# Attention steps of the first token tile placed ahead of the second tile's heads in a one-core transformer kernel

## What is computed

```python
n = _rms_norm(h, attn_norm[layer])
proj = n @ w_in[layer]
c_q, c_kv, k_rope, dq, dk, dv = jnp.split(proj, IN_SPLITS, axis=-1)
...
q = (_rms_norm(c_q, q_norm) @ w_uq).reshape(b, l, MLA_HEADS, MLA_QK_DIM)
kv = (_rms_norm(c_kv, kv_norm) @ w_ukv).reshape(b, l, MLA_HEADS, MLA_NOPE_DIM + MLA_V_DIM)
k_nope, v = kv[..., :MLA_NOPE_DIM], kv[..., MLA_NOPE_DIM:]
...
q = _rms_norm(q, qk_norm_q)
k = _rms_norm(k, qk_norm_k)
q = jnp.concatenate([q[..., :MLA_NOPE_DIM], _rope(q[..., MLA_NOPE_DIM:], pos)], axis=-1)
...
s = jnp.einsum('bqhd,bkhd->bhqk', qb, k) * scale
p = _causal_softmax(s, q_pos, pos)
return jnp.einsum('bhqk,bkhd->bqhd', p.astype(v.dtype), v)
...
mod = (c_act @ w_ada[l] + b_ada[l]).reshape(B, N_SUBLAYERS, N_MOD, D_MODEL)
```

## Time and profile before

| | us |
|---|---|
| median of 3 runs | 1675.62 |
| lowest and highest run | 1672.96 and 1677.15 |
| the profiled execution, its own time | 1671.1 |
| its span | 1669.2 |
| TensorE busy in it | 1290.4 |
| VectorE busy in it | 1021.7 |
| ScalarE busy in it | 402.0 |
| POOL busy in it | 572.4 |

### The profile page before, as it was taken

The page is one execution under the profiler, slowest core; times in us unless marked ns, Lnnn a source line. Parts: engine busy times, 40 slices in busy tenths (PEclk is TensorE's granted clock), DMA queues, the critical chain, the costliest instruction groups (busy, mean ns, idle before and its releaser), DMA issues.

```text
span 1669.2 us, 17159 instructions
## 1 busy us (share of the span) xinstructions
PE 1290.4 (77%) x6237; PEld 923.5 (55%) x6237; DVE 1021.7 (61%) x1897; ACT 402.0 (24%) x702; POOL 572.4 (34%) x626
## 2 busy tenths in 40 slices
PE   6987899687665554545565559999979889999997
PEld 3435667354222222222222226989969889799996
DVE  4575347977668577565655562767656554356655
ACT  1124312221001000110111101333334451144332
POOL 2100002677767767567777773101010000000000
PEclk9995589899777777777777779999989999899999
DMA  9634114899999999999999995777746435327561
GB/s 331 244 101 151 51 51 177 338 373 373 375 380 387 365 377 395 393 384 360 376 371 376 355 365 194 259 261 270 271 151 231 148 103 200 127 94 234 170 207 63
DMA packets 179707, 435.42 MB, mean 261 GB/s; under 512 B 13881, under 2 KB 84610, under 8 KB 179638
## 3 DMA queue, kind: packets, MB, share of 16 engines
q0 software_dynamic: 84384, 306.26, 48.4%
q1 hardware_dynamic: 94214, 126.18, 22.5%
q10 hardware_dynamic: 1040, 2.10, 0.4%
HBM read 433.44 MB, written 2.14 MB: 261 GB/s over the span
## 4 chain that ended last, share of the span: by engine, by line
PE 55%; DMA 14%; POOL 11%; DVE 10%; issue 7%; ACT 3%; SPq 0%; DVEq 0%; POOLq 0%; ACTq 0%
PE quad L1334 13%; PE quad_a L1292 7%; DMA arena<-in_peer_v_dram,arena 6%; PE quad_a L1348 6%; POOL ring L722 6%; PE quad L1292 5%; POOL arena L722 5%; PE quad_a L1077 5%; PE quad_a L1415 5%; DMA ring<-in_peer_v_dram,arena 4%; PE quad_a L1483 2%; PE quad L1152 2%; PE quad_a L1473 2%; DMA ring<-in_ffn_w_gu_dram 2%; PE quad L1235 1%
## 5 line engine op out<-in xcount | busy, mean ns | idle before, releaser
L1292 PE MATMUL quad_a<-arena 128*128 128x512 f32 x384 | 202.5, 692 | 158.6 <-DMA arena<-in_peer_v_dram,arena 158.6
L1292 PE MATMUL quad<-ring,arena 128*128 128x512 f32 x360 | 186.4, 681 | 119.3 <-DMA ring<-in_peer_v_dram,arena 119.3
L1292 PEld LDWEIGHTS quad_a<-arena 128*128 128x128 f32 x384 | 84.6, 226 | 275.9 <-issue 275.7
L722 POOL DMA_INDIRECT ring<-in_peer_u_dram,arena x136 | 138.5, 1018 | 247.5 <-PE quad L1152 178.2
L1334 PE MATMUL quad<-u_hi,w_hi 128*128 128x256 f32 x704 | 200.5, 285 | 2.7 <-DVE u_lo L1773 2.7
L1292 PEld LDWEIGHTS quad<-ring,arena 128*128 128x128 f32 x360 | 78.0, 222 | 224.6 <-issue 224.6
L1334 PE MATMUL quad<-u_lo,w_hi 128*128 128x256 f32 x704 | 200.4, 285 | 0.0
L1334 PE MATMUL quad<-u_hi,w_lo 128*128 128x256 f32 x704 | 200.2, 284 | 0.0
L1741 DVE TENSOR_TENSOR w_lo<-ring,w_hi 128x2048 fp32r<-128x2048 f32 x66 | 150.8, 2290 | 66.9 <-ACT w_hi L900 66.6
L675 POOL DMA_DIRECT2D arena<-in_w_ada_dram x48 | 25.4, 532 | 448.1 <-DVE arena L1542 445.5
L1873 DVE CUSTOM_DVE_ANT_0 arena<-ring,quad 128x1024 f32<-128x1024 f32 x128 | 154.8, 1221 | 25.2 <-DMA ring<-in_peer_u_dram,arena 16.9
(11 more groups left out here) (302 smaller groups left out, 2197.0 us busy)
## 6 DMA issues: line engine op xcount, KB each, us to landing
ring<-in_ffn_w_gu_dram SPq DMA_DIRECT2D x44, 1024.0 KB, 9.4
arena<-in_w_ada_dram POOLq DMA_DIRECT2D x48, 512.0 KB, 5.7
ring<-in_ffn_w_down_dram SPq DMA_DIRECT2D x22, 1024.0 KB, 4.9
ring<-in_w_mix_in_dram SPq DMA_DIRECT2D x20, 1024.0 KB, 6.3
ring<-in_w_ada_dram POOLq DMA_DIRECT2D x24, 512.0 KB, 5.5
arena<-in_peer_w_query_dram SPq DMA_DIRECT2D x4, 2048.0 KB, 8.2
arena<-in_w_in_dram SPq DMA_DIRECT2D x3, 2048.0 KB, 14.2
arena<-in_w_out_dram SPq DMA_DIRECT2D x2, 2048.0 KB, 10.3
```

The costliest lines, as they stand in the source:

```text
L722: gp.indirect_dma_start(out=rows_of(n), out_offset=None, in_=t["peer_" + kind][0], in_offset=bass.IndirectOffsetOnAxis(ap=expert[tt][:, sl ...
L1292: last = te.matmul(sum_side[tt][:, cols], diag[:, i % DIAGS], rows_of(n)[:, cols], start=(slot == pe_slots[0]), stop=(slot == pe_slots[-1] ...
```

## The change

Attention of tile 0 is begun once the latent heads of tiles 0 and 2 are turned, and other work is put between its steps.

- TensorE: after `cT` come the latent heads of tiles 0 and 2 at once, then `dq` of both tiles, `dv` of tile 0, and the turning of the latent heads of tiles 0 and 2. Then the loop begins. In pass 0, after the scores, stands `dv` of tile 1. In pass 1, after `o` of step 0, stand `dv` of tile 2, the turning of all differential heads, and the latent heads of tile 1. In pass 3, after `o` of step 2, stands the turning of tile 1's latent heads. The quarters of `keys` move from passes 1 to 4 to passes 3 to 6.
- VectorE: the latent heads of q0, k0 and k2 are done first, then those of `dq`. The sums of q1 and k1 stand at the end of pass 1, their scaling and rotation at the end of pass 2.
- ScalarE: its copies and roots follow.
- `v_row`, the rotation's scratch rows and `tmp` move to other places. The `w_ada` slices of this stage have three buffers instead of four, and their groups on VectorE are 6, 12 and 6, so 18 stand ahead of the copy of `cT` instead of 14. POOL's wait for the biases now stands ahead of the 19th load.
- SP: the load of `g_ffn` (512 KB) moves from the start to behind step 5 of attention; the loads of `w_out` and of the query weights wait for tile 1's heads.

```diff
-        v_row = area(arena, W2, 3 * MH * MV).rearrange("p (t n) -> p t n", t=3)
-        rot = area(arena, W2 + 3 * MH * MV, 3 * MH * ROPE).rearrange("p (s h c) -> p s h c", s=3, h=MH)
+        v_row = area(ring, 8960, 3 * MH * MV).rearrange("p (t n) -> p t n", t=3)
+        rot = [area(ring, at, MH * ROPE).rearrange("p (h c) -> p h c", h=MH) for at in (10496, 10752, 12032)]
         dv_row = area(arena, W2 + 2304, 3 * DH * DV).rearrange("p (t n) -> p t n", t=3)
...
-        tmp = area(ring, 4352, 1024)
+        tmp = area(ring, 11008, 1024)
...
-        ADA_BUFS = 4
-        ada_head = [area(ring, at, D) for at in (0, D, 2 * D, 9984)]
-        ada_late = [area(arena, LATE + D * i, D) for i in range(ADA_BUFS)]
+        ADA_HEAD, ADA_LATE = 3, 4
+        ada_bufs = [area(ring, D * i, D) for i in range(ADA_HEAD)] + [area(arena, LATE + D * i, D) for i in range(ADA_LATE)]
 
         def ada_buf(n):
 
-            return (ada_late if ADA[n][0] else ada_head)[n % ADA_BUFS]
+            return n % ADA_HEAD if n < 24 else ADA_HEAD + (n - 24) % ADA_LATE
+
+        def ada_turn(n):
+
+            return n // ADA_HEAD if n < 24 else (n - 24) // ADA_LATE
 
         def ada_count(s, columns):
...
         a_jobs = [("c", tt) for tt in range(3)] + [("rope", tt) for tt in range(3)] + [("dk", tt) for tt in range(3)]
-        a_jobs += [("dq", tt) for tt in range(QT)]
-        for tt in range(3):
+        for tt in (0, 2):
             a_jobs += [("q", tt, n) for n in range(2) if tt < QT] + [("kv", tt, n) for n in range(2)]
-        a_jobs += [("dv", tt) for tt in range(3)] + [("dkT", tt) for tt in range(3)] + [("dqT", tt) for tt in range(QT)]
-        for tt in range(3):
+        a_jobs += [("dq", tt) for tt in range(QT)] + [("dv", 0)]
+        for tt in (0, 2):
             a_jobs += [("qT", tt, n) for n in range(2) if tt < QT] + [("kT", tt, n) for n in range(2)]
+        a_jobs.append(("dv", 1))
         for i, (tt, g) in enumerate(STEPS):
-            if i < 4:
-                a_jobs.append(("keysT", i))
+            if 2 <= i < 6:
+                a_jobs.append(("keysT", i - 2))
             a_jobs += [("pT", i, m) for m in maps(g)]
+            if i == 0:
+                a_jobs += [("dv", 2)] + [("dkT", tt) for tt in range(3)] + [("dqT", tt) for tt in range(QT)]
+                a_jobs += [("q", 1, n) for n in range(2)] + [("kv", 1, n) for n in range(2)]
+            if i == 2:
+                a_jobs += [("qT", 1, n) for n in range(2)] + [("kT", 1, n) for n in range(2)]
 
         ADA_JOBS = ("columns", 0, 1)
...
             sp.dma_start(w_rope, w_in[:, :, C_ROPE:C_ROPE + ROPE]).then_inc(ld_rope_w, 16)
-            sp.dma_start(g_ffn, t["ffn_norm"].to_broadcast([P, D])).then_inc(ld_gffn, 16)
...
             sp.dma_start(keys, t["peer_sub_keys"][0].rearrange("h s n d -> n (h s) d")).then_inc(ld_keys, 16)
-            sp.wait_ge(a_full.sem, a_at["dqT", QT - 1] + 1)
-            sp.wait_ge(head_ready.sem, 1)
+            sp.wait_ge(a_full.sem, a_at["kv", 1, 1] + 1)
+            sp.wait_ge(head_ready.sem, 4)
             for n in range(2):
                 sp.dma_start(wo_half[n], w_out[:, :, n * 512:(n + 1) * 512]).then_inc(ld_wo, 16)
-            sp.wait_ge(a_full.sem, a_at["kT", 2, 1] + 1)
+            sp.wait_ge(a_full.sem, a_at["kT", 1, 1] + 1)
             load_query(1)
             sp.wait_ge(a_full.sem, a_at["keysT", 3] + 1)
             load_query(0)
+            sp.wait_ge(d_full.sem, d_at["o", 5] + 1)
+            sp.dma_start(g_ffn, t["ffn_norm"].to_broadcast([P, D])).then_inc(ld_gffn, 16)
             sp.wait_ge(d_full.sem, d_at["o", len(STEPS) - 1] + 1)
             load_query(2)
...
                     s, m, k = ADA[n]
-                    if n >= ADA_BUFS:
-                        pool.wait_ge(ada_used.sem, n - ADA_BUFS + 1)
+                    if ada_turn(n):
+                        pool.wait_ge(ada_used.sem, n - (ADA_LATE if s else ADA_HEAD) + 1)
                     src = t["w_ada_2"][0, k * P:(k + 1) * P, (3 * s + m) * D:(3 * s + m + 1) * D]
-                    gp.dma_start(ada_buf(n), src).then_inc(ld_ada[n % ADA_BUFS], 16)
+                    gp.dma_start(ada_bufs[ada_buf(n)], src).then_inc(ld_ada[ada_buf(n)], 16)
 
             def begin_sums(*sums_of):
...
             pool.wait_ge(d_full.sem, d_at["nT", 2, 1] + 1)
-            load_ada(*range(ADA_BUFS))
+            load_ada(*range(ADA_HEAD))
             bias_ready.step(pool, gp.memset(mask, 0.0))
             for tt in range(QT):
                 bias_ready.step(pool, gp.affine_select(out=mask[:, tt], in_=mask[:, tt], compare_op=ALU.is_ge, fill=NEG,
                                                        base=META + P * tt, pattern=[[-1, KEYS]], channel_multiplier=1))
...
 
-            load_ada(*range(10, 24))
+            load_ada(*range(18, 24))
...
+            evac_up(0)
+            evac_up(2)
+            evac_dq(0)
+            for name in (("q", 0), ("k", 0), ("k", 2)):
+                root(name, ROWS_OF.get(name, P))
+            evac_dq(1)
+            evac_dv(0)
+            evac_turned(0)
+            evac_turned(2)
+            for tt in range(QT):
+                root(("dq", tt))
...
+                if i == 0:
+                    evac_dv(1)
...
                     tt, g = STEPS[i - 1]
-                    if i < 5:
-                        n = i - 1
+                    if 3 <= i < 7:
+                        n = i - 3
                         evac(("keysT", n), lambda b: [(keysT[:, 4 * n:4 * n + 4], b[:, :].rearrange("p (s n) -> p s n", s=4))])
...
+                if i == 1:
+                    evac_dv(2)
+                    evac_diff()
+                    evac_up(1)
+                    for name in (("q", 1), ("k", 1)):
+                        root(name)
+                if i == 3:
+                    evac_turned(1)
...
-            pe.wait_ge(ld_dq, 16)
-            chunk("dq", w_slot[2], 512, range(QT))
-            pe.wait_ge(ld_up, 32)
-            for tt in range(3):
+            def up_heads(tt):
...
-            pe.wait_ge(ld_dv, 16)
-            chunk("dv", w_slot[0], 512, range(3))
-            for tt in range(3):
...
+            pe.wait_ge(ld_up, 32)
+            up_heads(0)
+            up_heads(2)
+            pe.wait_ge(ld_dq, 16)
+            chunk("dq", w_slot[2], 512, range(QT))
+            pe.wait_ge(ld_dv, 16)
+            chunk("dv", w_slot[0], 512, (0,))
+            turn_heads(0)
+            turn_heads(2)
...
-                    if i == 0:
-                        pe.wait_ge(a_free.sem, a_at["kT", 2, 1] + 1)
+                    if i in (0, 2, 4):
+                        pe.wait_ge(a_free.sem, a_at[{0: ("kT", 2, 1), 2: ("dqT", 1), 4: ("kT", 1, 1)}[i]] + 1)
...
+                if i == 0:
+                    chunk("dv", w_slot[0], 512, (1,))
...
-                if 1 <= i < 5:
-                    turn_keys(i - 1)
+                if 3 <= i < 7:
+                    turn_keys(i - 3)
...
+                if i == 1:
+                    chunk("dv", w_slot[0], 512, (2,))
+                    turn_diff()
+                    up_heads(1)
+                if i == 3:
+                    turn_heads(1)
...
-            sum_ada(4)
+            sum_ada(6)
...
-            sum_ada(10)
+            sum_ada(12)
...
             sum_ada(6)
             for tt in range(3):
                 half_heads("dk", tt, C_DK, dk_ready)
-            for tt in range(QT):
-                ve.wait_ge(a_free.sem, a_at["dq", tt] + 1)
-                half_heads("dq", tt, C_DQ, None)
-            sum_ada(4)
-            for tt in range(QT):
-                half_heads("dq", tt, C_DQ, dq_ready)
-
-            order = [("q", 0), ("k", 0), ("q", 1), ("k", 1), ("k", 2)]
             def heads(which, tt):
                 row = (q_row if which == "q" else k_row)[0:ROWS[tt], tt]
                 return row.rearrange("p (h c) -> p h c", h=MH)
-            for which, tt in order:
+
+            def head_sums(which, tt):
...
-            for which, tt in order:
+
+            def turned_heads(which, tt):
...
+            for which, tt in HEADS[:3]:
+                head_sums(which, tt)
+            for which, tt in HEADS[:3]:
+                turned_heads(which, tt)
+            for tt in range(QT):
+                ve.wait_ge(a_free.sem, a_at["dq", tt] + 1)
+                half_heads("dq", tt, C_DQ, None)
+            for tt in range(QT):
+                half_heads("dq", tt, C_DQ, dq_ready)
...
+                    if i == 1:
+                        for which, t in HEADS[3:]:
+                            head_sums(which, t)
+                    if i == 2:
+                        for which, t in HEADS[3:]:
+                            turned_heads(which, t)
```

72 lines of the change are left out of this document (36 added, 36 removed).

## The result

The median of 20 runs is 1681.22 us (1676.66 to 1689.79) against 1675.52 us for 20 runs of the kernel before (1664.03 to 1679.44), in the same comparison. The ratio is 1.0043, with a 95% interval of 1.0028 to 1.0058: 5.7 us by the medians, 7.2 us by the ratio, 4.7 to 9.7 us by its interval. The prediction was 1682, and +6.

The account below looks back on a forecast made before the run. Bounds: TensorE's waits for VectorE's latent heads, small products at 1.2 GHz, VectorE's earlier timeline and waits inside passes. Step 4 8.1 us later, +1.0 and -2.5 gave +6.6, taken as +6: 1675.6 + 6 = 1682 us, range 1666 to 1690.

Parts of the forecast that it names:

- Part 1: The way to `cT`: without `dq` as cover, TensorE waits 8.7 us from 67.4, where it had waited nothing.
- rounds of load and sum: Ahead of `cT`: nine `w_ada` slices in three rounds of three buffers, one taken at 10.0 us and two at 7.1.
- slow restart: TensorE at the latent heads, after the wait for `cT`: 1.5 us added for running at the lower clock.
- rival C: `w_ada` slices land in 3.8 us, `cT` is ready at 68.2, Part 2 is 7.9 us earlier: 1674 us; chance 0.13.
- Part 2: Latent heads of tiles 0 and 2: the first scores start at 112.7 instead of 138.35, 25.6 us earlier.
- VectorE and not TensorE sets the end here: End of the latent heads of tiles 0 and 2: VectorE's chain ends at 110.5, TensorE's at 108.4.
- Part 3: First scores to step 4's: 66.5 us against 32.7 before, as moved work comes back; 56.5 at full clock.
- filling: Between steps on TensorE: `dv` of tile 2, turning of differential heads, heads of tile 1, and 1.5 for the clock: 17.0 us.
- slow start: At scores 0, `dv` of tile 1 and scores 1: 1.7 us added, within a piece of 10.9 us.
- Part 4: After step 4's scores start: +1.0 us for `keys`, -2.5 for those scores at higher clock and what follows.
- Rival B: The filling keeps TensorE at 2.4 GHz, Part 3 is 56.5 us and the time 1670 us; chance 0.20.
- D: Rivals B and C both hold, full clock and early slices: 1662 us; chance 0.06.

Follow-up runs that it names:

- the three variants with the same beginning: The changed kernel with tile 1's heads a step up (1.0049), with turnings of no use (1.0008), or with VectorE's turning in its idle stretch (1.0000), against the kernel before.
- the second trace: The changed kernel run again without any edit, beside three variants on the same chip; ratio 1.0060 to the kernel before.
- the run that hid it: Changed kernel with VectorE's turning of tile 1's q and k heads moved up into its idle stretch of step 2; ratio 1.0000 to the kernel before.

## Why the prediction was right, step by step

- **`cT` loses its cover (Part 1).** Predicted 8.7 us of waiting; 9.43 and 10.35 in two traces, 7.05 to 8.94 in the three variants with the same beginning. The rounds of load and sum were as slow as taken: from the start of the ninth sum, 52.6, to the end of the 18th, 78.4, it took 25.8 us; predicted were 25.4. Round by round it was 9.9, 8.0 and 6.7 us for the predicted 10.0, 7.1 and 7.1. The slow restart cost 2.05 us (4.79 instead of 2.74), predicted 1.5.
  The page's row for these loads (count, size, median us to landing) is now this; it was 5.5 us before, and the other traces of the changed kernel and its variants with three buffers have 5.3 to 6.3:

```profile
ring<-in_w_ada_dram POOLq DMA_DIRECT2D x24, 512.0 KB, 6.2
```

  With it rival C fell. By the fit in the Trainium skill's "DMA: Bandwidth & Descriptors", section "Anatomy of one DMA — SWDGE (gpsimd) path", 2.0 us and the bytes at 436 GB/s, such a load would take 3.2 us, an estimate for a load on its own; none of the 24 loads of the earlier trace rows landed in under 3.8, and their median is 5.5.
- **First scores (Part 2).** Predicted 112.7, with 110 to 115 as the sign; 115.11, and 112.94 in the second trace. VectorE's terms were right one by one (sums 15.0 for 15.1, `dk` 2.5, three head sums 6.5, turning 9.4 for 9.4), and it ended 2.6 us late, of which 2.4 were there at the ninth sum (52.6 for 50.2). "VectorE and not TensorE sets the end here" did not hold in the changed kernel. TensorE ended `dv` of tile 0 at 111.7 (predicted 108.4) and then did the 24 turnings from 111.57 on without a pause, although VectorE ended the last head only at 113.1:

```profile
112.85 0.28 DVE L1682 TENSOR_TENSOR arena<-ring 16x128 f32<-16x128 f32 x1
```

  The same holds in the second trace and in three variants. It was nearly a tie: the prediction left out that 16 turnings, 2 us, stand ahead of the last head's, and its number did not suffer, since both chains wait for the same sums. In the runs with `cT` ahead of the sums and with seven buffers TensorE does wait for VectorE there (16.29 us, and 0.45 and 2.06 us). So the prediction was right that most of TensorE's wait is wait which VectorE's chain has in any case, and wrong on who came last.
- **From there to step 4 (Part 3).** Predicted 66.5 us; 66.50 and 64.97. By pieces, from the rows above: scores, `dv`, scores 9.1 (115.1 to 124.2; predicted 10.9), softmax until the output 3.5 (3.5), output 4.9 (4.0), filling 17.9 (17.0), until output 1 7.3 (6.9), output 1 4.9 (5.0), until `pT` of step 2 10.5 (10.4), it and output 2 4.0 (4.2), turning 4.4 (4.6). The exact sum is partly luck: no slow start behind the turned heads (-1.7), and a clock that fell already at 127.4 for the output and the filling (+1.8). That VectorE's turning was 5.8 of the 7.92 us of waiting is shown by the run that hid it.
- **The rest of attention (Part 4).** Predicted -1.5 against the kernel before's 65.5 us. It was 66.6 in the first trace (+1.1) and 63.1 in the second (-2.4). Step 4's scores took 3.99 us in one and 2.10 in the other, at half and at full clock. In the trace of every variant of the changed kernel these scores took 2.10 too; the first trace is the exception. So the term is about as large as was said, and in a single trace it can be missing.
- **The clock.** Predicted 0.50 from about 150 until step 5; it was 0.51 from 154.8 to 186. The 0.51 from 127.4 to 137.6 was not among the signs, though the sum had 4.0 us for the output and 1.5 us in the filling for a slower clock. Rival B had 1.00 throughout; the filling did raise the clock, but it lasted for 17 us only. With 66.5 us for Part 3 instead of 56.5, B fell, and D with it.
- **The sum.** +6 predicted, +5.7 measured by the medians and +7.2 by the ratio, within +4.7 to +9.7; beside the experiments the ratio of 1.0060 makes it 10 us (6.2 to 14.5). The traces have +11.7 and +4.4 at the end of attention, and +9.3 and +6.0 counted from the latent turnings, for a forecast of +6.6. So the mechanism and its size are borne out, and that the medians hit within 0.3 us is luck. One slip in the chances: half of B's 0.20 is 0.10 and not 0.09.

What stays open: why the clock falls in one execution and not in the next where TensorE's work is the same, and how much of the change's price lies behind attention, where traces of these kernels differ by more than the price.

## What to carry to other kernels

Before an operation is moved away, ask which late arrival it covers; here a product of 14 us hid a copy that was 10 us late. A step that starts early is worth only as much as the chain behind it doesn't give back: the moved work came back whole, in TensorE's order and once more on VectorE, which had stood idle for 7 us with the work ready, and did it just when it was waited for; one place further up in its queue it cost 6 us less. And a load that must wait for its buffer stops when its user stops: more buffers, taken from columns that are used later, were worth some 10 us, where taking the copy ahead of the sums cost 12 to 15.

## What the hardware showed that was not expected

- Work of no use on TensorE, placed in its waits, made the kernel before 13 us faster (0.9923), without moving anything else.
- The granted clock falls to 0.50 also while TensorE is busy: for 6.2 us from 140.7, of which it worked 5.91, behind 18.7 us in which it had worked 13.55.
- The same instructions ran at 0.53 for 3.5 us in one execution and at 1.00 in another. Six traces of kernels whose order on TensorE is the same up to there reach the latent turnings at 64.40 to 68.84 us. A trace alone can't tell 3 us here.
